# Four projections of a two-layer streaming encoder in seven products instead of eight, with scans moved ahead of query copies

## What is computed

```
proj = rms(x, norm_mix) @ w_in
(..., m_q, m_k, m_v, m_o, m_if) = split(proj)              # 256 columns each, m_if 8
y_d = mlstm(m_q, m_k * HEAD_DIM ** -0.5, m_v, i, logsig(f), C, n, m)
y_d = head_rms(y_d, on) * sigmoid(m_o)
```

## Time and profile before

| | us |
|---|---|
| median of 3 runs (lowest to highest) | 928.33 (928.27 to 928.68) |
| the profiled execution | 928.3 |
| its span | 926.5 |
| busy: PE, DVE, ACT, POOL | 920.3, 498.6, 209.9, 444.4 |

### The profile page before, as it was taken

One profiled execution on the slowest core, in us unless ns is written; L12 is line 12 of the kernel. 1 busy time (PEld: TensorE's weight loads), 2 busy tenths in 40 slices (PEclk: granted clock), 3 DMA queues, 4 the chain that ended last, 5 costly groups with the idle time before them and its releaser, 6 DMA issues.

```text
span 926.5 us, 14897 instructions
## 1 busy us (share of the span) xinstructions
PE 920.3 (99%) x5712; PEld 812.7 (88%) x5712; DVE 498.6 (54%) x1018; ACT 209.9 (23%) x457; POOL 444.4 (48%) x469
## 2 busy tenths in 40 slices
PE   8999999999999999999999999999999999999998
PEld 6777877778999999999977678777799999999998
DVE  6674656845565656512363665577356556563221
ACT  3224255432000000100132244462310011100001
POOL 6210380125966666676411215403268666666670
PEclk9999999999999999999999999999999999999999
DMA  9969312129555554433434673112655555533321
GB/s 280 237 131 98 112 46 92 52 17 251 138 139 141 142 141 144 134 129 126 133 124 136 30 147 96 47 48 50 138 150 141 143 142 143 147 125 126 131 94 39
DMA packets 159636, 113.02 MB, mean 122 GB/s; under 512 B 10247, under 2 KB 157357, under 8 KB 159437
## 3 DMA queue, kind: packets, MB, share of 16 engines
q1 hardware_dynamic: 154660, 104.50, 39.0%
q0 software_dynamic: 4272, 6.80, 7.3%
q10 hardware_dynamic: 632, 0.75, 0.3%
HBM read 108.46 MB, written 2.27 MB: 120 GB/s over the span
## 4 chain that ended last, share of the span: by engine, by line
PE 98%; DMA 1%; ACT 0%; SPq 0%; DVE 0%; issue 0%; DVEq 0%; ACTq 0%
PE ps L1133 52%; PE ps L785 20%; PE ps L1090 8%; PE ps L1151 2%; PE ps L891 1%; PE ps L860 1%; PE ps L987 1%; PE ps L927 1%; PE ps L1028 1%; PE ps L1037 1%; PE ps L813 1%; PE ps L833 1%; PE ps L970 1%; DMA arena<-in_x_sample 1%; PE ps L1048 1%; PE ps L1069 0%
## 5 line engine op out<-in xcount | busy, mean ns | idle before, releaser
L785 PE MATMUL ps<-hT,ring 128*128 128x320 f32 x608 | 169.4, 434 | 0.3 <-DVEq L433 0.3
L602 POOL TENSOR_TENSOR work<-ring 128x512 f32<-128x512 f32 (+1 forms) x66 | 81.8, 1239 | 153.7 <-issue 113.4
L785 PEld LDWEIGHTS ps<-hT,ring 128*128 128x128 f32 x608 | 113.7, 190 | 45.6 <-DVEq L433 0.8
L1133 PE MATMUL ps<-mixT,ring 128*128 128x160 f32 x672 | 105.0, 299 | 0.0
L1133 PE MATMUL ps<-hT,work 128*128 128x160 f32 x672 | 98.5, 299 | 0.0
L1133 PE MATMUL ps<-hT,ring 128*128 128x160 f32 x672 | 98.1, 299 | 0.0
L1133 PEld LDWEIGHTS ps<-mixT,ring 128*128 128x128 f32 x672 | 95.8, 190 | 0.0
L1133 PEld LDWEIGHTS ps<-hT,ring 128*128 128x128 f32 x672 | 93.7, 190 | 0.3
L1133 PEld LDWEIGHTS ps<-hT,work 128*128 128x128 f32 x672 | 93.7, 190 | 0.0
L604 POOL TENSOR_TENSOR work<-ring 128x512 f32<-128x512 f32 (+1 forms) x66 | 82.4, 1248 | 5.2
L603 POOL TENSOR_TENSOR ring<-ring 128x512 f32<-128x512 f32 (+1 forms) x66 | 82.2, 1246 | 5.2
(11 more groups left out here) (398 smaller groups left out, 1389.9 us busy)
## 6 DMA issues: line engine op xcount, KB each, us to landing
ring<-in_w_gu SPq DMA_DIRECT2D x88, 512.0 KB, 5.2
ring<-in_w_in SPq DMA_DIRECT2D x44, 512.0 KB, 7.2
ring<-in_w_down SPq DMA_DIRECT2D x32, 512.0 KB, 4.4
ring<-in_w_out SPq DMA_DIRECT2D x16, 512.0 KB, 4.4
ring<-in_w_down SPq DMA_DIRECT2D x16, 384.0 KB, 3.4
cst<-in_consts POOLq DMA_DIRECT2D x1, 1664.0 KB, 12.2
ring<-in_w_in SPq DMA_DIRECT2D x2, 640.0 KB, 5.5
arena<-r POOLq DMA_DIRECT2D x8, 160.0 KB, 17.4
```

What stands on the lines that cost most here:

```text
L602: step(tt(s3, a11, a21, ALU.subtract))
L785: ins = mm(bank(use, 0, T, m), w[:, k, c:c + m], right[:, k, 0:T], start=(k == 0), stop=(k == KT - 1))
L1133: ins = mm(bank(use, at * HT, HT), left, right(k), start=(opens and k == 0 and at == 0), stop=(closes and k == n - 1), skip_group_check=True)
```

## The change

The projections `mo`, `mv`, `mq` and `mk` are computed by seven products of four matmuls each over 160 frames, instead of two times eight matmuls over 320. GpSimd mixes the four weights (`pair_weights`): those of `mo` and `mv` ahead of its first stores of the layer, those of `mq` behind the store of the rotated keys, those of `mk` behind the broadcasts of the gate rows. VectorE makes four sums of the normalised input (`half_sums`) right behind the query latents; ScalarE copies out each first product (`pair_first`), and VectorE adds the rest (`pair_result`). Results are in SBUF from then on: ScalarE copies the queries to heads from there, and the keys with their factor. On VectorE the scans of the gate rows and the values' additions stand ahead of the query copies, the state table ahead of the output gate, and the tables of lambda between queries and keys. On TensorE the values are transposed behind `qt2` instead of ahead of `qt0`. The banks of the uses are renamed, and `pair_t` is new in SBUF. `mo` has the order of the FFN's first unit (a product that needs no mixed weights is taken ahead), the other three the order of its other units.

```diff
-    d("ql0", "ql1", "kvr", "mo0", "mo1", "mgt", "mv0", "mv1")
-    u += [("cnT", (4,)), ("qms", (5,))]
-    d("mvt0", "mvt1")
-    u += [("qt0", (6,)), ("qt1", (7,)), ("qt2", (2,))]
-    d("mq0", "mq1", "mk0", "mk1")
+    d("ql0", "ql1", "kvr")
+    u += [("moa", (2,)), ("mob", (6,)), ("moc", (1,)), ("mgt", (0,)), ("mva", (5,)), ("mvb", (7,)), ("mvc", (4,))]
+    u += [("cnT", (6,)), ("qms", (0,)), ("qt0", (1,)), ("qt1", (2,)), ("qt2", (6,)), ("mvt0", (5,)), ("mvt1", (7,))]
+    u += [("mqa", (4,)), ("mqb", (0,)), ("mqc", (3,)), ("mka", (1,)), ("mkb", (2,)), ("mkc", (7,))]
+    dense[0] = 0
...
+        hp = mixT[:, :, :].rearrange("p k n -> p (k n)").rearrange("p (s k n) -> p s k n", s=4, k=4)
...
+        pair_t = sb("pair_t", [P, 4 * HT])
+        pair_p1, pair_u2, pair_u34 = pair_t[:, 0:HT], pair_t[:, HT:T], pair_t[:, T:2 * T]
...
+            def pair_weights(l, i):
+                name = PAIRS[i]
+                w, _ = quarters(name, l)
+                s2, s3, s4 = (pair_sums[i % 2][:, s] for s in range(3))
+                if i < 2:
+                    wait_filled(pool, ("ql1", "kvr")[i], l)
+                    if l == 0 and i == 1:
+                        pool.wait_ge(sem("rows_turned"), 3)
+                else:
+                    wait_used(pool, PAIRS[i - 2], l)
+                wait_chunk(pool, name, l)
+                a11, a12, a21, a22 = w[:, :, 0, 0, :], w[:, :, 1, 0, :], w[:, :, 0, 1, :], w[:, :, 1, 1, :]
+                tt = nc.gpsimd.tensor_tensor
+                step(tt(s3, a11, a21, ALU.subtract))
+                step(tt(a21, a21, a22, ALU.add))
+                step(tt(s2, a21, a11, ALU.subtract))
+                step(tt(s4, a12, s2, ALU.subtract), "mixed")
...
+                for i in range(2):
+                    pair_weights(l, i)
                 need(pool, "ckv_new", l, 1)
...
+                pair_weights(l, 2)
                 need(pool, "m_rows", l, 1)
...
+                pair_weights(l, 3)
                 need(pool, "q_ready", l, 1)
...
+            def feature_pair(name, l):
+                i = PAIRS.index(name)
+                w, _ = quarters(name, l)
+                s2, s3, s4 = (pair_sums[i % 2][:, s] for s in range(3))
+                a, b_, c = f"{name}a", f"{name}b", f"{name}c"
+                def one(use, at, left, right, opens=False):
+                    for k in range(KT // 2):
+                        ins = mm(bank(use, at * HT, HT), left(k), right(k), start=(opens and k == 0),
+                                 stop=(k == KT // 2 - 1), skip_group_check=True)
+                    return ins
+                def half(jj, t):
+                    return lambda k: hT[:, 2 * k + jj, t * HT:(t + 1) * HT]
+                def half_sum(n):
+                    if i == 0:
+                        need(pe, "h_sums", l, 8, n)
+                    return lambda k: hp[:, n - 1, k, :]
+                wait_chunk(pe, name, l)
+                claim(pe, a, l)
+                if i > 0:
+                    need(pe, "mixed", l, MADE, i + 1)
+                    one(a, 0, lambda k: w[:, k, 0, 0, :], half(0, 0), True)
+                    one(a, 2, lambda k: w[:, k, 1, 0, :], half(1, 0))
+                    fill(one(a, 1, lambda k: s2[:, k, :], half_sum(3)), a)
+                    claim(pe, b_, l)
+                    one(b_, 0, lambda k: w[:, k, 0, 1, :], half_sum(1), True)
+                    fill(one(b_, 1, lambda k: s3[:, k, :], half_sum(2)), b_)
+                    claim(pe, c, l)
+                    one(c, 0, lambda k: s4[:, k, :], half(1, 1), True)
+                    fill(one(c, 1, lambda k: w[:, k, 1, 1, :], half_sum(4)), c)
+                    return
+                one(a, 0, lambda k: w[:, k, 0, 0, :], half(0, 0), True)
+                one(a, 2, lambda k: w[:, k, 1, 0, :], half(1, 0))
+                claim(pe, c, l)
+                one(c, 1, lambda k: w[:, k, 1, 1, :], half_sum(4), True)
+                claim(pe, b_, l)
+                need(pe, "mixed", l, MADE, i + 1)
+                one(b_, 0, lambda k: w[:, k, 0, 1, :], half_sum(1), True)
+                fill(one(b_, 1, lambda k: s3[:, k, :], half_sum(2)), b_)
+                fill(one(a, 1, lambda k: s2[:, k, :], half_sum(3)), a)
+                fill(one(c, 0, lambda k: s4[:, k, :], half(1, 1)), c)
...
-                for p in range(2):
-                    feature(f"mo{p}", l, "mo", p * P, P)
...
+                feature_pair("mo", l)
...
-                for p in range(2):
-                    feature(f"mv{p}", l, "mv", p * P, P)
+                feature_pair("mv", l)
...
-                for p in range(2):
-                    value_tiles("mv", l, p)
...
+                for p in range(2):
+                    value_tiles("mv", l, p)
...
+                    pe.wait_ge(sem("ct_ready"), 1)
+                feature_pair("mq", l)
+                feature_pair("mk", l)
...
+                def pair_first(name):
+                    i = PAIRS.index(name)
+                    if i > 0:
+                        need(act, "pair_made", l, NPAIR, i)
+                    wait_filled(act, f"{name}a", l)
+                    step(A(pair_p1, bank(f"{name}a", 0, HT), ACT.Copy), "p1_copied")
+                pair_first("mo")
...
+                pair_first("mq")
+                need(act, "pair_made", l, NPAIR, 3)
+                for n in range(4):
+                    rs = slice(n % 2 * HD, n % 2 * HD + HD)
+                    step(A(qh[rs, n, :], raw[rs, n // 2, :], ACT.Copy), "mq_ready")
+                pair_first("mk")
+                if l == 0:
+                    act.wait_ge(sem("lam"), 1)
+                    A(lamt[:, 1, :], lamt[:, 0, :], ACT.Exp, scale=-1.0).then_inc(sem("lam_exp"), 1)
+                key_stats(range(3), KTILES - 3)
...
+                need(act, "pair_made", l, NPAIR, 4)
                 for p in range(2):
-                    wait_filled(act, f"mk{p}", l)
-                    step(A(kf[:, p, 0:T], bank(f"mk{p}", 0, T), ACT.Copy, scale=0.125), "mk_ready")
-                    now_read(act, f"mk{p}")
-                key_stats(range(3), KTILES - 3)
-                need(act, "gate_arg", l, 2)
+                    step(A(kf[:, p, 0:T], raw[:, 2 + p, :], ACT.Copy, scale=0.125), "mk_ready")
...
+                def half_sums():
+                    h_at = lambda j, t: hT[:, j::2, t * HT:(t + 1) * HT]
+                    step(v.tensor_tensor(hp[:, 0], h_at(0, 1), h_at(0, 0), ALU.subtract), "h_sums")
+                    step(v.tensor_tensor(hp[:, 1], h_at(1, 1), h_at(0, 1), ALU.subtract), "h_sums")
+                    step(v.tensor_tensor(hp[:, 2], h_at(1, 1), hp[:, 0], ALU.subtract), "h_sums")
+                    step(v.tensor_tensor(hp[:, 3], h_at(1, 0), hp[:, 2], ALU.subtract), "h_sums")
+                def pair_result(name):
+                    a, b_, c = (f"{name}{x}" for x in "abc")
+                    p1, u2, u34 = pair_p1, pair_u2, pair_u34
...
+                    halves = lambda x: x.rearrange("p (k n) -> p k n", k=2)
+                    need(dve, "p1_copied", l, P1S, PAIRS.index(name) + 1)
+                    step(v.tensor_tensor(u2, p1, bank(a, HT, HT), ALU.add))
+                    step(v.tensor_tensor(c11, p1, bank(a, 2 * HT, HT), ALU.add), bank_read=(a, l))
+                    wait_filled(dve, b_, l)
+                    step(v.tensor_tensor(halves(u34), halves(bank(b_, 0, T)), u2.unsqueeze(1).broadcast_to([P, 2, HT]), ALU.add))
+                    step(v.tensor_tensor(c22, u34[:, HT:T], bank(b_, 0, HT), ALU.add), bank_read=(b_, l))
+                    wait_filled(dve, c, l)
+                    if name == "mo":
+                        step(v.tensor_tensor(mid, halves(u34), halves(bank(c, 0, T)), ALU.add), bank_read=(c, l))
+                        step(v.tensor_scalar(pair_out[name], pair_out[name], SIG_MIN, None, ALU.max), "pair_made")
+                    else:
+                        step(v.tensor_tensor(mid, halves(u34), halves(bank(c, 0, T)), ALU.add), "pair_made")
+                        now_read(dve, c)
+                def scans():
...
+                    step(v.tensor_scalar(nm[:, 0:T], mro[:, :], -1.0, None, ALU.mult), "m_rows")
...
+                half_sums()
...
+                if l == 0:
+                    state_tables()
+                pair_result("mo")
...
-                if l == 0:
-                    state_tables()
-                    lam_tables()
                 need(dve, "kvr_gif_done", l, 2, 2)
                 step(v.scalar_tensor_tensor(out=lfr[:, :], in0=gff[:, :], scalar=0.0, in1=lfr[:, :],
                                             op0=ALU.min, op1=ALU.subtract))
+                scans()
+                pair_result("mv")
...
-                one = C("ones", H)[:, 0:1]
...
-                step(v.tensor_scalar(nm[:, 0:T], mro[:, :], -1.0, None, ALU.mult), "m_rows")
...
-                for p in range(2):
-                    wait_filled(dve, f"mq{p}", l)
-                    for a in range(2):
```

(20 more changed lines are left out.)

70 lines of the change are left out of this document (41 added, 29 removed).

## The result

| | median us (lowest to highest) | runs |
|---|---|---|
| kernel before, beside it | 928.50 (928.27 to 929.46) | 4 |
| changed kernel | 944.31 (943.67 to 945.24) | 4 |

The ratio is 1.0169, 95% interval 1.0151 to 1.0187: the change makes the kernel slower by 1.7%. The forecast was 939.5 with a range to 943.0. The direction and the mechanism were as forecast, but the time lies 1.3 us outside the range. The profiled execution took 943.9 us, its span is 942.1, and that of before 926.5: 15.6 us to explain.

A forecast was written before the change was run, and what follows sets the result against it. TensorE held 98% of the span, its savings counting only as far as VectorE keeps up. 928.3 + 7.5 (layer 0) + 2.6 (layer 1) + 1.0 (clock) = 939.4, rounded to 939.5 us; range 929.5 to 943.0, about 80%.

The forecast's parts named there:

- held-back operations: VectorE beside GpSimd's mixing: each mixing operation holds back one operation with both inputs in SBUF by about 1.0 us.
- the clock: TensorE's slow restart after standing still: bounds 0 and 2.0 us, taken as 1.0, on the path in layer 1.
- the last difference of the working for layer 0: Broadcast gate exponentials at 90.9 where they were at 82.79, so scores later and layer 0 +7.5 us.
- TensorE's gain: Each projection falls from 8.6 to 7.6 us, 56 records of 0.136: 4.0 us per layer, 8.1 for both.
- the likeliest case: Contention in all two-input VectorE operations, scans included: 936.5 to 942.5 us, 55% chance.
- The rest of layer 0: VectorE's work after the values' additions at 61.1, through queries, lambda tables and keys, to gate exponentials at 90.9.
- The wait for bank 2: Layer 0: the keys' additions free the bank at 82.9, and TensorE wants it for the gate broadcast at 79.5.
- Layer 1: Waits of 1.7 and 5.1 us, less 4.0 and 0.5, plus 0.3: +2.6 us, before the clock's share.
- Only wide operations wait: Rival: scans and 4-partition operations pass; layer 0 +4.8, layer 1 about 0, total 933.1 us; 22% chance.
- VectorE keeps up: Rival: nothing held back, or GpSimd's operations fall between VectorE's; layer 1 gains 4.1 to 4.4, total 923.9 us; 13% chance.
- GpSimd's own time: The mixing on GpSimd costs nothing; if late, it would be with the keys' weights, by about 1 us.
- later yet: Rival: both waits bring a slow restart, or mixing slows and the keys' weights are late too: 943 to 947 us, 6%.

The follow-up runs named there:

- experiment 1: Changed kernel without GpSimd's mixing for the four projections, whose products take unmixed quarters of the weights: 926.99 us, ratio 0.9982 to the kernel before.
- experiment 2: Changed kernel with only the queries' weights left unmixed, their products taking unmixed quarters: 933.55 us, ratio 1.0055 to the kernel before.
- experiment 5: Changed kernel plus matmuls that nothing reads, 28 in layer 0 and 18 in layer 1, before the values' transposes: 942.06 us, ratio 1.0146.
- experiment 3: Changed kernel with the scans of the gate rows moved back behind the query copies: 946.06 us, ratio 1.0190 to the kernel before.
- kernel 9: Changed kernel with scans back, earlier mixing, lambda tables and gate sigmoid moved, query copies on ScalarE, `mo` in the other projections' order: 923.86 us, ratio 0.9955.

## Why the prediction was right or wrong

**The step that failed** is the size of terms in the sum; the mechanism, held-back operations of VectorE that make TensorE wait, was right. The largest single error is the clock: in layer 1 the slow restart was put at 1.0 us, the middle of its bounds, and measured 1.85. In layer 0 seven held-back operations were counted ahead of the values' last addition, 7.0 us, and they measured 7.6: the half sums 2.7 where 1.0 was counted for one of them, the scans and the row operation 4.35 instead of 4.0, the latent sum 0.6 and the square nothing. And the last difference of the working for layer 0 was carried as 7.5 us where it is 8.1. Of the 4.8 us between 939.5 and 944.3 layer 0 makes 2.5 and layer 1 makes 2.0; the rest is that the profiled execution lies 0.4 below the median, less the rounding of the forecast.

**TensorE's gain** was right. The output gate's 56 records begin at 34.11 in layer 0 and the next matmul at 41.72, 0.136 us each.

**The held-back operations** were the right cause, for the scans too: the likeliest case had them wait, and experiments 1 and 2 show it. Three half sums of layer 0 were held back where the prediction counted one (VectorE; 0.83 unhindered):

```profile
26.39 1.64 DVE L1807 TENSOR_TENSOR mixT<-hT 128x640 f32<-128x640 f32 x1
28.06 0.83 DVE L1808 TENSOR_TENSOR mixT<-hT 128x640 f32<-128x640 f32 x1
28.92 1.77 DVE L1809 TENSOR_TENSOR mixT<-hT,mixT 128x640 f32<-128x640 f32 x1
30.73 1.77 DVE L1810 TENSOR_TENSOR mixT<-hT,mixT 128x640 f32<-128x640 f32 x1
```

They end at 32.50, not at 30.4; 0.4 of that is a later start. More than half of it came back, as a square that was forecast to be held back was not and the latent sum was held back by 0.6 instead of 1.0: the forget gate ended at 51.82, where 51.0 was forecast. The scans and the row operation were held back by 4.35 instead of 4.0, and the last addition of the values ended at 62.30 instead of 61.1: a wait of 7.76 us, not 6.6.

**The rest of layer 0.** The order of the late things was right, down to the tables of lambda (75.7 to 83.1, 7.4 us, as forecast). The keys' additions ended at 85.25, not 83.4, and the gate exponentials at 92.96, not 90.9: 1.2 us are the term above, 0.5 small steps among the queries, the rest in the keys' row. The wait for bank 2 was 0.36 us and not 3.4, as TensorE itself was later, mostly by the longer wait and the slow restart; both lie under VectorE's row, so the sum did not need it. And the working had a slip: from 82.79 to 90.9 are 8.1 us, and I carried 7.5. With the filler of experiment 5 TensorE was early enough, and the wait was 3.00. Layer 0 lost 10.04: 2.1 us of the miss are the later exponentials, 0.6 the slip, less 0.2 by which the scores follow them more closely than before.

**Layer 1.** Forecast were 1.7 for the half sums, 5.1 for the values, 1.0 for the clock, 0.3 at the gates, less 4.5 (4.0 of products and an old wait of 0.5). Measured are 1.86, 5.23, 1.85 (0.7 in the transposes, 1.15 in the next sixteen records) and 0.62 before the scores, 9.56 in all; as layer 1 lost 5.60, 3.96 were saved. The difference of 2.0 is the clock (0.85), the saving (0.54), the gates (0.32) and the two waits (0.29). The clock was the term to take at its upper bound: the one start in the trace gave 2.0, and both long waits cost 1.8 and more.

**The rivals.** "Only wide operations wait" (933.1) falls with the scans' rows and with experiment 2. The argument against it, that 160 and 320 columns wait equally, had no row among the groups; the trace of before bears it out roughly, as an addition of 128x160 beside mixing takes 1.05 us in the median and 0.32 at least, and one of 128x320 takes 1.15 and 0.49 (L2144, L2155). "VectorE keeps up" (923.9) is what experiment 1 comes near to, 927.0: layer 0 is then 2.5 us behind before, by the wait for bank 2 behind the tables (2.34 us), and layer 1 gains 3.7. That GpSimd's own time costs nothing held in the changed kernel, and experiment 3 shows that TensorE's waits were the cover.

**The range** ended too low: it took 1.0 us as the most that one hold could cost, where the scans show up to 1.5, and the clock of layer 1 in the middle of its bounds, and added nothing for both being worse at once. The case "later yet" (943 to 947), which had 6%, is where the time fell, by larger holds, the slow restart in layer 1 and the slip, not by late weights. Both waits did bring a slow restart, as that case has it, but the one of layer 0 cost nothing. The direction came from the mechanism. The size owes a little to luck: a square of layer 0 that was counted as held back was not, which hid 1.0 us of the half sums.

## What to carry to other kernels

Before work is given to GpSimd beside VectorE, list VectorE's operations in that stretch that read two operands from SBUF, whatever their width, and count for each GpSimd operation that runs beside them one held back by up to about its length (0.6 to 1.5 us here, each operation of GpSimd taking 1.27); then see who waits for that row. Place the new work where VectorE reads PSUM or stands idle, and see to it that a wait which is removed does not show the next one (here the waits for mixed weights), by moving both at once. The product form itself was no loss: the same four projections in seven products gave +1.7% in one placement of the work around them and -0.5% in another.

## What the runs showed of the hardware

- The hold is mutual. Beside VectorE's half sums of 0.83 us, GpSimd's mixing took 1.72 to 1.73 us instead of 1.27, and the half sums 1.77; scans of 4 partitions and an operation of 128 x 4 were held back as well, by 0.9 to 1.5 us. (The Trainium skill, SBUF — State Buffer, "Who interferes with whom", says that whoever has the shared pair of ports has it for the whole instruction. The rows agree.) GpSimd beside the last half sums, and once they are done:

```profile
30.08 1.73 POOL L618 TENSOR_TENSOR ring<-ring 128x512 f32<-128x512 f32 x1
31.89 1.73 POOL L619 TENSOR_TENSOR work<-ring 128x512 f32<-128x512 f32 x1
33.70 1.28 POOL L620 TENSOR_TENSOR work<-ring,work 128x512 f32<-128x512 f32 x1
```

- One hold comes ahead of the record that should explain it. The first half sum of layer 0 ran from 26.39 to 28.03 and took 1.64 us, though the first mixing is on record from 28.29. Without mixing, with the same loads issued beside it, it took 0.83 (experiment 1). So the loads' issues held nothing back. In kernel 9 it took 0.83 too, with the first mixing on record 0.26 us behind its end. How an operation that is on record only later could hold it back, and why it did not in kernel 9, the traces do not show.
- Filler matmuls that nothing reads can be worth their place in a wait, where TensorE stands still for other reasons and its slow restart is on the path. The 18 in layer 1 gained 1.8 us; the 28 in layer 0 gained 0.2, as a later wait took up what they saved.
